# A fused decoder layer on eight cores: finer hazard buffers, other step costs in the build-time order, and another split of the last blocks

## The reference

```python
h   = x @ w_in + b_in                       # 5632 columns: q, k, v, z, gate_a, gate_g
y_a = sliding_window_attention(q, k, v, sinks) @ w_br_a   # 16 heads, 4 kv heads, window 128
y_g = (u * (tril(W_s) LN(v') + b_s)) @ w_br_g             # u, v' = split(gelu(z)), chunks of 128
mix = sigmoid(gate_a) * y_a + sigmoid(gate_g) * y_g
x   = layer_norm(ALPHA * x + mix @ w_out, ln1)
x   = layer_norm(ALPHA * x + relu(x @ w_up)**2 @ w_down, ln2)     # d_ff = 4096
```

## Time and profile before

| | us |
|---|---|
| runs | 1038.11, 1236.2, 1037.97; median 1038.11 |
| the profiled execution, own time | 1037.65 |
| its span, slowest core (the eight: 1035.0 to 1036.1) | 1036.1 |
| PE busy | 1004.8 (97%) |
| DVE, ACT, POOL busy | 589.8, 380.6, 101.3 |
| granted TensorE clock, mean | 0.995 to 0.996 on all cores |

### The profile page before, as it was taken

The page is one execution under the profiler, slowest core; times in us unless marked ns, Lnnn a source line. Parts: engine busy times, 40 slices in busy tenths (PEclk is TensorE's granted clock), DMA queues, the critical chain, the costliest instruction groups (busy, mean ns, idle before and its releaser), DMA issues.

```text
span 1036.1 us, 16955 instructions; the slowest of 8 cores (1035.0 to 1036.1 us)
## 1 busy us (share of the span) xinstructions
PE 1004.8 (97%) x5792; PEld 491.3 (47%) x5902; DVE 589.8 (57%) x1226; ACT 380.6 (37%) x578; POOL 101.3 (10%) x163
## 2 busy tenths in 40 slices
PE   9999999999999999999999999999999999999995
PEld 3446455554444444444444645555444444444442
DVE  3866577765776312444676837777486842134454
ACT  0456566641325200331134645666223430023221
POOL 4210000000111000000023000000010100010015
PEclk9999999999999999999999999999999999999998
DMA  9995243253787902954299222632366564086012
GB/s 163 194 174 97 42 66 58 42 114 84 148 144 147 151 8 44 163 78 83 85 181 149 47 41 42 106 60 42 102 137 128 86 127 73 1 137 107 9 74 82
DMA packets 20630, 98.85 MB, mean 95 GB/s; under 512 B 2369, under 2 KB 3265, under 8 KB 12098
## 3 DMA queue, kind: packets, MB, share of 16 engines
q0 software_dynamic: 13200, 73.14, 45.2%
q1 hardware_dynamic: 7346, 24.61, 7.2%
HBM read 162.50 MB, written 8.39 MB: 165 GB/s over the span
## 4 chain that ended last, share of the span: by engine, by line
PE 90%; DVE 5%; issue 2%; ACT 1%; DVEq 0%; POOL 0%; ACTq 0%; POOLq 0%
PE ps L443 58%; PE ps L1206 21%; PE ps L696 3%; DVE scr L948 2%; PE ps L977 1%; PE ps L936 1%; PE ps L552 1%; ACT regK L415 1%; PE ps L836 1%; PE ps L998 1%; PE ps L1123 1%; PE ps L1029 1%; PE ps L1219 1%; DVE lnbuf L401 1%; DVE scr L404 1%
## 5 line engine op out<-in xcount | busy, mean ns | idle before, releaser
L443 PE MATMUL ps<-reg,ring 128*128 128x512 bf16 x1500 | 340.9, 379 | 2.4 <-issue 0.7
L443 PE MATMUL ps<-xT_s,ring 128*128 128x512 bf16 (+1 forms) x1060 | 245.6, 377 | 5.3 <-DVE den L1012 2.9
L443 PEld LDWEIGHTS ps<-reg,ring 128*128 128x128 bf16 x1536 | 147.4, 98 | 174.7 <-issue 3.9
L1206 PE MATMUL ps<-ring,reg 128*128 128x512 bf16 x972 | 213.7, 379 | 1.1
L415 ACT ACTIVATE scr<-ps 128x512 f32<-128x512 f32 x128 | 76.5, 597 | 262.8 <-PE ps L443 253.6
L443 PEld LDWEIGHTS ps<-xT_s,ring 128*128 128x128 bf16 x1104 | 103.1, 98 | 116.1 <-issue 6.8
L1206 PEld LDWEIGHTS ps<-ring,reg 128*128 128x128 bf16 x992 | 97.1, 98 | 117.0
L404 DVE SCALAR_TENSOR_TENSOR reg<-ps,scr 128x512 bf16<-128x512 f32 x128 | 87.7, 690 | 113.6 <-ACT scr L415 113.4
L948 DVE CUSTOM_DVE_ANT_1 scr<-ps,lnbuf 128x384 f32<-128x384 f32 x128 | 71.1, 555 | 51.2 <-PE ps L936 31.7
L415 ACT ACTIVATE scr<-scr,amx 128x384 bf16<-128x384 f32 x128 | 78.5, 613 | 37.1 <-DVE amx L404 30.0
L471 POOL DMA_DIRECT2D ring<-wst x62 | 34.2, 555 | 446.8 <-PE ps L443 177.3
(11 more groups left out here) (104 smaller groups left out, 824.3 us busy)
## 6 DMA issues: line engine op xcount, KB each, us to landing
ring<-wst POOLq DMA_DIRECT2D x62, 1024.0 KB, 10.5
regK<-x SPq DMA_DIRECT2D x16, 512.0 KB, 5.6
y<-scr SPq DMA_DIRECT2D x15, 512.0 KB, 3.0
lnbuf<-lnrep SPq DMA_DIRECT2D x4, 1024.0 KB, 9.4
xT_s<-xt POOLq DMA_DIRECT2D x2, 1024.0 KB, 20.9
ring<-wz POOLq DMA_DIRECT2D x2, 1024.0 KB, 10.4
xT_s<-xt POOLq DMA_DIRECT2D x7, 256.0 KB, 18.8
ring<-wz POOLq DMA_DIRECT2D x7, 256.0 KB, 14.9
```

The costliest lines, as they stand in the source:

```text
L443: r = e.matmul(out, lhsT=a, rhs=b, start=(k == 0), stop=(k == 7))
L1206: r = e.matmul(ps[:, b2 + half, :], lhsT=hreg[fi // 8][:, th, fi % 8, bb * 128:(bb + 1) * 128], rhs=wd[quarter][:, fi % 4, half * 512:(hal ...
```

## The change

Five edits, all in the builder of the program:

1. `schedule`: other delays between engines, and a new delay `own_after` for a dependency on the same engine (0.19 for ACT, 0.185 for DVE, 0.15 for POOL, where it was 0).
2. The costs of the simulated operations are replaced, mostly by smaller ones.
3. Finer buffers: `parts` makes fresh `Buf`s that come after an older one. The root has its own (`B_rs`), separate from mean and variance; bn_stats halves, the two maxima of a unit (`B_mx`), their combination (`B_nm`), the two halves of the exponentials and the eight slices of `Cg` have their own.
4. Blocks 4 to 6 of the last group: DVE computes (x - mean) * g into a separate tile before the root is known, ACT multiplies by the root, and b is added in two halves of 512 columns, both by POOL in blocks 4 and 5, one by POOL and one by DVE in block 6. In the other blocks of this norm the same first DVE operation no longer needs the root, and the operation that writes the mean to column 12 is gone.
5. The last block: four column pieces (512, 256, 128, 128) in four banks in place of three, with 30 floats of bn_stats in place of 24; the operations with (x - mean) * g get a lead and need no root.

The diff, cut to what is spoken of:

```diff
-seen_after = {"pe": 0.3, "act": 0.2, "dve": 0.15, "pool": 0.2, "sp": 0.2}
+seen_after = {"pe": 0.27, "act": 0.2, "dve": 0.2, "pool": 0.25, "sp": 0.2}
+own_after = {"pe": 0.0, "act": 0.19, "dve": 0.185, "pool": 0.15, "sp": 0.0}
...
-                at = max(at, t if d.dma else t if d.eng == e else t + seen_after[d.eng])
+                at = max(at, t if d.dma else t + own_after[e] if d.eng == e else t + seen_after[d.eng])
...
-B_amx = [Buf("amx%d" % i) for i in range(3)]
+B_rs = [None] * NST
+B_mx = [[[Buf("mx") for _ in range(2)] for _ in range(4)] for _ in range(3)]
+B_nm = [[Buf("nm") for _ in range(4)] for _ in range(3)]
...
-    return 0.17 + width(ap) / 940.0
+    return 0.075 + width(ap) / 950.0
+
+def act_cost(ap):
+    return 0.105 if width(ap) <= 16 else 0.22 + width(ap) / 1430.0
+
+def parts(n, after):
+
+    new = [Buf("part") for _ in range(n)]
+    Prog.alias_after(new, after)
+    return new
...
+    hb = parts(2, [b])
     for h in halves:
-        timed(P.op("dve", (lambda h: lambda e: e.bn_stats(out=t[:, h * 6:h * 6 + 6], in_=src[:, h * 512:(h + 1) * 512]))(h), reads=R, writes=[b]), 0.79)
+        timed(P.op("dve", (lambda h: lambda e: e.bn_stats(out=t[:, h * 6:h * 6 + 6], in_=src[:, h * 512:(h + 1) * 512]))(h), reads=R, writes=[hb[h]]), 0.61)
     if 1 in halves:
-        ahead(timed(P.op("dve", lambda e: e.bn_aggr(out=t[:, 12:14], in_=t[:, 0:12]), reads=[b], writes=[b]), 0.31))
-        ahead(ts(t[:, 14:15], t[:, 13:14], eps, ALU.add, [b], [b]))
-        timed(P.op("pool", lambda e: e.tensor_tensor(out=t[:, 15:16], in0=t[:, 14:15], in1=mhalf[:, 0:1], op=ALU.pow),
-                   reads=[b, C["mhalf"]], writes=[b]), 0.7)
+        ahead(timed(P.op("dve", lambda e: e.bn_aggr(out=t[:, 12:14], in_=t[:, 0:12]), reads=hb, writes=[b]), 0.13))
+        root(s, t[:, 13:14], eps)
     return s
+
+def root(s, var, eps, by=0.5):
+
+    t, b = lst[:, s, :], B_st[s]
+    pv, B_rs[s] = parts(2, [b])
+    ahead(ts(t[:, 14:15], var, eps, ALU.add, [b], [pv]), by)
+    ahead(timed(P.op("pool", lambda e: e.tensor_tensor(out=t[:, 15:16], in0=t[:, 14:15], in1=mhalf[:, 0:1], op=ALU.pow),
+                     reads=[b, pv, C["mhalf"]], writes=[B_rs[s]]), 0.75), by)
...
-        mv = ms[:, 0:768].rearrange("p (s a n) -> p s a n", s=2, a=2)
+        mv = ms.rearrange("p (s r) -> p s r", s=2)[:, :, 0:384].rearrange("p s (a n) -> p s a n", a=2)
         for sub in range(2):
             o = P.op("dve", (lambda sub: lambda e: e.tensor_tensor_reduce(
                 out=mv[:, sub], in0=ps[:, 0:2, sub * 192:(sub + 1) * 192], in1=mk[:, sub].unsqueeze(1).broadcast_to([128, 2, 192]),
                 scale=1.0, scalar=-3.0e38, op0=ALU.add, op1=ALU.max, accum_out=mx[:, 2 * bb + sub:2 * bb + sub + 1]))(sub),
-                reads=[B_ps[0], B_ps[1], C["masks"]], writes=[bms[0] if sub == 0 else bms[1], B_amx[ai]])
-            o.cost = 0.65
+                reads=[B_ps[0], B_ps[1], C["masks"]], writes=[bms[sub], B_mx[ai][bb][sub]])
+            o.cost = 0.5
         stt(mx[:, 8 + 2 * bb:10 + 2 * bb], mx[:, 2 * bb:2 * bb + 2], -0.125, negsk4[:, hk:hk + 1].broadcast_to([128, 2]), ALU.mult, ALU.min,
-            [B_amx[ai], C["sinks"]], [B_amx[ai]])
-        pt, bpt = h1(4 + rot("P", 3))
+            B_mx[ai][bb] + [C["sinks"]], [B_nm[ai][bb]])
+        pt, bslot = h1(4 + rot("P", 3))
+        bpt = parts(2, bslot)
         p16 = pt.bitcast(BF16)[:, 0:768].rearrange("p (a n) -> p a n", a=2)
         for sub in range(2):
-            act(p16[:, :, sub * 192:(sub + 1) * 192], mv[:, sub], AF.Exp, bms + [B_amx[ai]], bpt,
-                bias=mx[:, 8 + 2 * bb + sub:9 + 2 * bb + sub], scale=0.125)
-        cx[t].update(p16=p16, bpt=bpt)
+            act(p16[:, :, sub * 192:(sub + 1) * 192], mv[:, sub], AF.Exp, [bms[sub], B_nm[ai][bb]], [bpt[sub]],
+                bias=mx[:, 8 + 2 * bb + sub:9 + 2 * bb + sub], scale=0.125).cost = 0.52
+        cx[t].update(p16=p16, bpt=bpt + bslot)
...
-                for ip, (c0, n) in enumerate(((0, 512), (512, 256), (768, 256))):
-                    bk = b2 if ip == 0 else b2 + 1 if ip == 1 else B_extra
+                pieces = br2
+                fb = parts(5, [B_fin])
+                for ip, (c0, n, i0) in enumerate(((0, 512, 0), (512, 256, 2), (768, 128, 3), (896, 128, 4))):
+                    bk = (b2 + ip) % 8
                     dcol(blk, bk, c0, n)
                     cs = slice(c0, c0 + n)
-                    ahead(tt(r2[:, cs], xb_[:, cs], ps[:, bk, 0:n], ALU.add, [B_x1[blk], B_ps[bk]], [br2[c0 // 512]]), 1.0 if ip else 0.4)
-                    for c1 in range(c0, c0 + n, 256):
-                        i = c1 // 256
-                        ahead(timed(P.op("dve", (lambda i, c1: lambda e: e.bn_stats(out=bn[:, i * 6:i * 6 + 6], in_=r2[:, c1:c1 + 256]))(i, c1),
-                                         reads=[br2[c0 // 512]], writes=[B_fin]), 0.45), 1.0 if ip else 0.4)
-                ahead(timed(P.op("dve", lambda e: e.bn_aggr(out=t[:, 12:14], in_=bn), reads=[B_fin], writes=[B_st[sl]]), 0.31), 1.0)
-                ahead(ts(t[:, 14:15], t[:, 13:14], EPS, ALU.add, [B_st[sl]], [B_st[sl]]), 1.0)
-                ahead(timed(P.op("pool", lambda e: e.tensor_tensor(out=t[:, 15:16], in0=t[:, 14:15], in1=mhalf[:, 0:1], op=ALU.pow),
-                                 reads=[B_st[sl], C["mhalf"]], writes=[B_st[sl]]), 0.7), 1.0)
+                    pb = [br2[0]] if ip == 0 else parts(1, [br2[1]])
+                    ahead(tt(r2[:, cs], xb_[:, cs], ps[:, bk, 0:n], ALU.add, [B_x1[blk], B_ps[bk]], pb), 1.0 if ip else 0.4)
+                    if ip:
+                        pieces.append(pb[0])
+                    for i, c1 in enumerate(range(c0, c0 + n, 256), i0):
+                        ahead(timed(P.op("dve", (lambda i, c1, w_: lambda e: e.bn_stats(out=bn[:, i * 6:i * 6 + 6], in_=r2[:, c1:c1 + w_]))(i, c1, min(n, 256)),
+                                         reads=pb, writes=[fb[i]]), 0.08 + min(n, 256) / 950.0), 1.0 if ip else 0.4)
+                ahead(timed(P.op("dve", lambda e: e.bn_aggr(out=t[:, 12:14], in_=bn), reads=fb, writes=[B_st[sl]]), 0.13), 1.0)
+                root(sl, t[:, 13:14], EPS, 1.0)
...
-                    stt(r2[:, hs], r2[:, hs], t[:, 12:13], lnbuf[:, 0, hs], ALU.subtract, ALU.mult, [br2[half], B_st[s], B_ln], [br2[half]])
+                    ahead(stt(r2[:, hs], r2[:, hs], t[:, 12:13], lnbuf[:, 0, hs], ALU.subtract, ALU.mult,
+                              ([br2[0]] if half == 0 else br2[1:]) + [B_st[s], B_ln], [br2[half]]), 1.0)
                 for half in range(2):
                     hs = slice(half * 512, (half + 1) * 512)
-                    stt(r2[:, hs], r2[:, hs], t[:, 15:16], lnbuf[:, 1, hs], ALU.mult, ALU.add, [br2[half], B_st[s], B_ln], [br2[half]])
+                    stt(r2[:, hs], r2[:, hs], t[:, 15:16], lnbuf[:, 1, hs], ALU.mult, ALU.add, [br2[half], B_st[s], B_rs[s], B_ln], [br2[half]])
...
+                hh, bhh = h2(10) if spread(blk) else (r2, br2)
+                ahead(stt(hh, r2, t[:, 1:2], lnbuf[:, 0, :], ALU.add, ALU.mult, br2 + [B_st[s], B_ln], bhh), 0.2 if spread(blk) else 0.0)
                 if spread(blk):
-                    ahead(tt(t[:, 3:4], t[:, 1:2], t[:, 15:16], ALU.mult, [B_st[s]], [B_st[s]], eng="pool"))
-                    act(r2, r2, AF.Identity, br2 + [B_st[s]], br2, bias=t[:, 3:4], scale=t[:, 15:16])
-                    tt(r2, r2, lnbuf[:, 0, :], ALU.mult, br2 + [B_ln], br2, eng="pool").cost = 2.4
-                    tt(r2, r2, lnbuf[:, 1, :], ALU.add, br2 + [B_ln], br2, eng="pool" if blk < NB - 2 else "dve").cost = 2.4 if blk < NB - 2 else 1.3
+                    act(r2, hh, AF.Copy, bhh + [B_st[s], B_rs[s]], br2, scale=t[:, 15:16])
+                    for half in range(2):
+                        hs = slice(half * 512, (half + 1) * 512)
+                        on_dve = blk == NB - 2 and half == 1
+                        tt(r2[:, hs], r2[:, hs], lnbuf[:, 1, hs], ALU.add, [br2[half], B_ln], [br2[half]],
+                           eng="dve" if on_dve else "pool").cost = 0.61 if on_dve else 1.2
                 else:
-                    ln_affine(r2, br2, s, r2, br2)
+                    stt(r2, r2, t[:, 15:16], lnbuf[:, 1, :], ALU.mult, ALU.add, br2 + [B_st[s], B_rs[s], B_ln], br2)
```

More of the change, by code:

```diff
@@ L304, in build_program @@
         lst = sb("lst", [128, NST, 16])
-        fin = sb("fin", [128, 24])
+        fin = sb("fin", [128, 30])
         B_fin = Buf("fin")
@@ L338, in build_program @@
         B_keep = [Buf("kk"), Buf("kv")]
-        C = {n: Buf(n) for n in ("bcol", "hgate", "brow", "ident", "sinks", "wsT", "tril", "Cg", "wsTb", "masks", "mhalf", "ones", "warm")}
+        C = {n: Buf(n) for n in ("bcol", "hgate", "brow", "ident", "sinks", "wsT", "tril", "wsTb", "masks", "mhalf", "ones", "warm")}
+        B_Cg = [Buf("Cg%d" % i) for i in range(8)]
         def h2(i):
@@ L410, in ts @@
```

(31 more changed lines are left out.)

6 lines of the change are left out of this document (3 added, 3 removed).

## The result

The changed kernel takes **1023.07 us** (median of 4 runs, 1022.69 to 1023.36); a second set of its runs gave 1022.80. Times from here on are medians of the executions in which the cores of neither die were slowed; a few others took up to 19% longer, at a lower granted clock. The ratio to the kernel before is **0.9855, 95% interval 0.9836 to 0.9875**: 1.45% faster, well clear of zero. That is under the 2% which the prediction took as the least that a measurement can tell; the interval shows that far less can be told. The prediction was 1031.5, between 1026 and 1038; the kernel is faster than the range's lower end by 2.9.

A forecast was written before the change was run, and what follows sets the result against it. PE, busy 97% of the span, was taken as the bound, so only its standing time could be won. Tail 3.4, attention 2.3 and spatial 0.9 sum to 6.6 us, giving 1031.5 us, range 1026 to 1038.

The forecast's parts named there:

- Attention (edits 1 to 3): Attention stretches: separate `amx` buffers save 0.14 per unit, shortening PE's waits; 2.3 us won, between nothing and 7.7.
- The new order itself: Whole program, edits 1 and 2: can remove at best the listed waits, 9.5 us, or add as many; zero taken.
- Tail: Behind the last product, edits 3 to 5: a shorter DVE chain wins 3.4 us, between 1.3 and 4.1.
- the second rival: Tail: POOL's additions hold DVE again, striking block 6's first operation; up to 1.2 us lost, 1032.7; chance 0.08.
- The spatial stretch: Stretch with spatial products: independent `Cg` slices finish 1.4 us earlier, PE gains 0.9, between 0 and 1.8.
- separate buffers are worth nothing on DVE: Rival for attention and spatial stretch: separate buffers gain nothing on DVE, only the tail moves; 1034.7 us, chance 0.22.
- All waits for DVE go: Rival: all waits for DVE in attention and the spatial products vanish, 9.5 + 3.4 off; 1025.2 us, chance 0.10.
- the slower rival: Attention: cheaper costs put S products ahead of what DVE delivers, blocking PE; 6.2 us slower, 1044.3; chance 0.12.

The follow-up runs named there:

- Experiments 6 and 7: Changed kernel, old costs and delays, one kind of shared-`amx` wait put back: first maximum on ACT's earlier exponentials, 1026.25 us; DVE's waits on itself, 1026.10 us.
- b_costs: Kernel before with only the new costs and delays, all buffers and the tail old; 1026.82 us, ratio 0.9887.
- d_coarse: Changed kernel with one `amx` buffer for four units again, the exponentials' halves keeping their own; 1026.01 us, ratio 0.9878.
- p_act: Changed kernel with block 7's root made by ACT's square root and DVE's reciprocal in place of POOL; 1021.56 us, ratio 0.9831.
- a_attbuf: Kernel before with only the separate attention buffers; costs, delays and tail old; 1027.83 us, ratio 0.9897.
- e_oldcosts: Changed kernel with the old costs and delays in the planner, buffers and tail new; 1023.96 us, ratio 0.9858.
- p_both: Changed kernel with block 7's root on ACT and DVE, and both halves of block 6's addition on POOL, each stored by itself; 1022.69 us, ratio 0.9838.
- b1_delays: Kernel before with only the new delays, between engines and on the same engine; costs, buffers and tail old; 1055.35 us, ratio 1.0162.

## Why the prediction was wrong

**The failed step: "Attention (edits 1 to 3)", 2.3 taken, 10.3 measured.** I costed the shared `amx` by the pair of maxima alone, 0.14 per unit. The same name stands in the exponentials' reads and in the writes of the next unit's maxima, so in this bookkeeping the first maximum of a unit also waits for ACT's exponentials of the unit before. The bracket of the first row says so, and I passed over it: DVE was idle 0.55 for ACT. The S product and the exponentials around it, before:

```profile
138.03 0.34 PE L936 MATMUL ps<-regK,reg 64*128 64x192 bf16 x4
...
138.76 1.31 ACT L415 ACTIVATE scr<-scr,amx 128x384 bf16<-128x384 f32 x2
...
141.86 1.31 ACT L415 ACTIVATE scr<-scr,amx 128x384 bf16<-128x384 f32 x2
```

The S product is issued at 138.03, and its first maximum starts at 140.21, 0.14 after the exponentials end (140.07). Maximum, maximum, combination, exponentials and the next maximum are thus one chain: from 140.21 through the next exponentials, which end at 143.17, to 143.31 with the same 0.14, it is 3.1 long (this next maximum started at 143.38, behind another operation of DVE). The period of a unit with PE never waiting is 3.12 (96.59 over 31): the chain had no slack. A unit after:

```profile
171.72 0.34 PE L957 MATMUL ps<-regK,reg 64*128 64x192 bf16 x4
171.89 1.11 ACT L429 ACTIVATE scr<-scr,amx 128x384 bf16<-128x384 f32 x2
172.20 0.56 DVE L969 CUSTOM_DVE_ANT_1 scr<-ps,lnbuf 128x384 f32<-128x384 f32 x1
...
172.78 0.53 DVE L969 CUSTOM_DVE_ANT_1 scr<-ps,lnbuf 128x384 f32<-128x384 f32 x1
```

The first maximum starts 0.48 after the S product and in the middle of the exponentials; the second follows after 0.58. Experiments 6 and 7 fit such a chain: either part put back costs 2.1 to 2.3, both 8.1, more than their sum, as when two parts together outgrow the period. That the chain is the reason is argued from these numbers. Not separated is how much of it the buffers bring on the chip and how much through the order that is made from them, since no run held the order fixed.

**"The new order itself", zero taken.** It is a second cure that works by itself: 6.5 of the 10.3 with the buffers as they were (`b_costs`). The start times of S products suggest how: before, 12 and 9 of 31 of a group's S products were issued within 0.8 us of the start of the second maximum of the unit before, that is, as soon as the banks were free, and PE stood still for them; with the new costs 3 and 4, with the buffers none. The count is not all of it: `d_coarse` has 7 and 7 and loses less than `b_costs` (3.1 against 3.8). I had the mechanism among the rivals, as one that makes it *slower*; it worked the other way. Zero between two bounds of 9.5 was no finding, and the bounds belonged in the range.

**The gain that waits can give was read too small.** I took 9.5, the listed waits, as all that could be won among the products; 12.5 was won. Attention alone lost 10.3, where I counted 7.7 of waits and called the rest "gaps of hundredths". PE's list has three more lines there, which the earlier trace rows left out:

```profile
PE ps L443 <- issue: 1.0, 6, 0.3
PE ps L998 <- DVE lnbuf L401: 0.6, 3, 0.3
PE ps L977 <- ACT bes L415: 0.2, 1, 0.2
```

With them the list has 9.5 in attention. The stretches miss 11.5 of busy PE, about 10 without the gaps of missing records. And a busy matmul is shown 0.38 long while the next can start after 0.216, so a stall under 0.16 leaves no gap at all. The window of counted work, used above, needs neither.

**Tail: 3.4 predicted, 2.1 measured.** DVE's chain did what was forecast:

```profile
1009.78 1.95 PE L1241 MATMUL ps<-ring,reg 128*128 128x128 bf16 x32
...
1011.84 0.29 DVE L415 TENSOR_TENSOR scr<-reg,ps 128x128 f32<-128x128 f32 x1 [0.21 <-PE ps L1241]
1012.23 0.29 DVE L1276 BATCH_NORM_STATS2 fin<-scr 128x6 f32<-128x128 f32 x1
1012.63 0.29 DVE L1278 BATCH_NORM_AGGREGATE lst<-fin 128x2 f32<-128x30 f32 x1
1013.40 0.15 DVE L423 TENSOR_SCALAR lst<-lst 128x1 f32<-128x1 f32 x1 [0.48 <-DVE lst L1278]
1013.47 1.40 DVE L418 SCALAR_TENSOR_TENSOR scr<-scr,lst,lnbuf 128x512 f32<-128x512 f32 x2
1013.70 0.92 POOL L652 TENSOR_TENSOR lst<-lst,mhalf 128x1 f32<-128x1 f32 x1 [2.30 <-DVE lst L423]
1014.79 0.69 DVE L415 TENSOR_TENSOR scr<-scr,lnbuf 128x512 f32<-128x512 f32 x1
1015.39 1.41 DVE L418 SCALAR_TENSOR_TENSOR scr<-scr,lst,lnbuf 128x512 f32<-128x512 f32 x2
```

Against the earlier trace rows: the first of the four operations starts 0.07 after the start of var + eps, and the first two no longer wait for the root; all four take 1.40 and 1.41 per pair, the 2.75 is gone; the last pair ends at 1016.80, 5.1 behind the last product, where the last store was issued 8.4 behind it. That is 3.3 won of 3.4 on DVE's path. But DVE's path does not set the end: "its store at 1032.62, which sets the end" was true before by 0.3 on this core (POOL's multiplication ended at 1028.89, and 6.93 more is 1035.8) and by as little on one other; on the remaining six the span ended 6.94 behind POOL's multiplication already. After, POOL's root is the last to count. 1.3 of the gain were left standing, and `p_act` fetched it: its span ends 8.2 behind the last product, where 8.5 was forecast. One part of the 1.3 is the 0.48 in which DVE stood idle between aggregation and var + eps: the kernels with the new last blocks in which this step is 0.11 end 9.45 behind the last product, 0.37 sooner. (The prediction's end of block 6's half on POOL, 1024.1, is also not the sum of the terms that it gives, which make 1023.4; only the margin of the second rival hung on it.)

**The spatial stretch: 0.9 predicted.** The listed 1.8 are gone, and the first S comes 1.2 earlier, 1.9 in the median of the cores. Here, too, there are two causes. That median is 106.4 before and in `a_attbuf`, 105.4 in `e_oldcosts` (all finer buffers, old costs), 104.6 in `b_costs` (new costs, one buffer for the slices) and 104.5 after. So the finer buffers outside attention bring the forecast 0.9 by themselves, and the costs 1.8, which was not forecast. How much of the 0.9 is the `Cg` slices was not isolated; the waits of the spatial products are 1.4 in `a_attbuf` and 0.4 in `e_oldcosts`.

**The rivals.** That separate buffers are worth nothing on DVE fell with `a_attbuf`. By the Trainium skill (VectorE: DVE Perf Modes, "The DRAIN you can't avoid") a semaphore between chained DVE operations is free; the trace does not agree for operations that need not be chained: the two maxima start 0.71 apart with a shared buffer and 0.58 apart without in the unit above. That POOL holds DVE did not happen in the changed kernel, as no long POOL operation ran then: none of the tail's operations of 512 columns took over 0.8. By the Trainium skill (SBUF — State Buffer, "Who interferes with whom") the later of the two waits; the 2.75 before agrees. So does `p_both`: DVE's first operation took 1.31 from 1013.97 while POOL's half ran to 1014.73, and ended 0.55 behind it. "All waits for DVE go", with 0.10, is what happened, and its 1025.2 was still 2.1 too high, as it was worked out from the listed waits. An order that loses time exists, as the slower rival had it, but came only with half of the edit (`b1_delays`), and there most waits stand at transposes and products with V, not at S.
